# Feed-forward up and gate products: the two rounded parts of the tokens side by side as one 512-column moving operand, the halves added on the way out

## The chip, the cores and the metric

The kernel runs on one core of a Trainium2 chip. The metric is the device time of one execution in microseconds. Engines are named as in the profile: PE is TensorE's matmul side, PEld its weight loads, ACT is ScalarE, DVE is VectorE, SP is SyncE, whose queue issues the loads from memory.

## The reference

Two transformer stacks run one after the other on 256 tokens of width 1024 (the second stack adds 16 meta tokens). The change touches only the feed-forward blocks of the first stack: two layers with two blocks each, four in all.

```python
D_MODEL = 1024; SEQ = 256; DEPTH = 2; D_FF = 2816

def swiglu(h, w_in, w_out):
    gate, up = jnp.split(h @ w_in, 2, axis=-1)
    return (jax.nn.silu(gate) * up) @ w_out
```

Everything is float32. The rest (token mixing with a gated delta rule and sparse attention, then attention, a recurrence and two mixtures of experts in the second stack) is left as it is.

## The kernel before

The program is a list of stages; the four feed-forward stages are called FFN 0 to FFN 3 here (from 36.8, 486.7, 686.4 and 1130.9 us of the span). All weights come as a stream of 1 MB slabs through a ring of `RING = 8` slots, and SP issues the load of slab i when the reader of slab i-8 has signalled. The ring and the order of the slabs are fixed by `slab_plan`.

A float32 product is made of three products of rounded operands (type fp32r): `w = w_hi + w_lo` and `v = v_hi + v_lo`, where the `hi` part is the value rounded by a copy and `lo` is what is left, and `w_hi*v_hi + w_hi*v_lo + w_lo*v_hi` is accumulated in PSUM. `thirds` issues these three matmuls (lines 1523, 1524, 1525), each with 128x128 weights and 256 moving columns (the tokens).

A feed-forward stage has `FFN_STEPS = 11` steps, and step t has 256 of the 2816 hidden columns. For each step:

- SP loads a `gate`, an `up` and a `down` slab, and 0, 1 or 2 `ada` slabs, which carry the modulation weights of later stages (FFN 0, 1 and 2 carry 16 of them: two in each of the steps 0 to 5, one in 6 to 9; FFN 3 carries 4).
- ACT rounds each of the three slabs (`split_hi`, L1673), DVE subtracts to get the low part (`split_lo`, L3123). DVE also sums the `ada` slabs (`sum_slab`, L739), two instructions and two short ones a slab, and thereby frees their slots (`ada_sum`).
- PE runs `up_split(t+1)` and then `down_split(t)`. `up_split` makes two units u = 2t and 2t+1 of 128 hidden columns; a unit is gate and up (j = 0, 1) over 8 pieces k of the width, 16 calls of `thirds`, 48 matmuls. `down_split` is 16 calls, 48 matmuls. So a step has 144 matmuls, a stage 1584.
- For each unit ACT computes silu of the gate half (L2155) and DVE multiplies it with the up half and splits the product (`hidden_split`, L3132, L3133, L3134), which signals `hid_done`.

PSUM has eight banks. Unit u uses bank u % 3, gate in columns 0 to 255 and up in 256 to 511; the sums of `down_split` stay in banks 3 to 6. The queues are in order, and DVE's order inside step a is: three `split_lo`, `hidden_split(a+1)`, the sums of the `ada` slabs of step a. ACT's is three `split_hi`, then the two silu. The slab order makes the `up` and `down` slabs of a later step wait for these sums: in the steps with two `ada` slabs, the load of the `down` slab that is split before `hidden_split(a+1)` is released by the second `ada_sum` after `hidden_split(a)`. The wait on PE in `up_split` is

```python
if u >= 3:
    pe.wait_ge(s["hid_done"], u - 2)
```

which is: unit u may start when unit u-3 has been read. `down_split(t)` waits for both units of its own step.

## Time and profile before

| | us |
|---|---|
| median of 3 runs | 2811.76 (2811.54 to 2816.03) |
| the profiled execution, its own time | 2810.16 |
| its span | 2808.3 |
| FFN 0, 1, 2, 3 on PE, first to last matmul of `thirds` | 36.8 to 229.5, 486.7 to 678.6, 686.4 to 876.9, 1130.9 to 1321.5 |

In the profile a line's mean duration of a matmul is longer than the distance between two starts, since matmuls are pipelined; the distance between starts is what counts in a stream.

### The profile page before, as it was taken

Reading aid. Unit: us, or ns where it says so; the run is one execution under the profiler, and the core shown is the slowest. Engines: PE = TensorE matmul, PEld = TensorE weight load, DVE = VectorE, ACT = ScalarE, POOL = GpSimd, SP = SyncE. Lnnn points to the kernel's source line nnn. Section 1 sums busy time; section 2 is a strip of 40 time slices with the busy share of each in tenths; the row PEclk is TensorE's granted clock in tenths of the full one; section 3 lists DMA queues with packets and bytes.
Section 4 is the critical chain, followed back from the end, with each engine's and each line's share of the span. In section 5 each row is a group of like instructions: output and inputs, shape, how many; then the busy total and the mean of one; then the engine's idle time right before and its main releaser. Section 6 shows DMA issues by size and latency. Waiting matters only on the chain.

```text
span 2808.3 us, 44780 instructions
## 1 busy us (share of the span) xinstructions
PE 2630.2 (94%) x18742; PEld 1900.3 (68%) x18742; DVE 1388.0 (49%) x2815; ACT 771.1 (27%) x1471; POOL 0.2 (0%) x4
## 2 busy tenths in 40 slices
PE   7999988999999988999999999999999999999998
PEld 6998867999999877999777533333357784333333
DVE  7875864786774774763233333333324541333333
ACT  3332443334342352442233211111012321111010
POOL 0000000000000000000000000000000000000000
PEclk8999989999999999999999999999999999999999
DMA  8776311675775411554211599999961237999997
GB/s 346 309 280 260 125 46 61 255 286 207 295 292 214 149 61 35 197 220 165 75 63 44 209 376 428 427 427 428 427 270 61 91 121 278 422 428 427 427 428 329
DMA packets 72353, 701.51 MB, mean 250 GB/s; under 512 B 8784, under 2 KB 11472, under 8 KB 11728
## 3 DMA queue, kind: packets, MB, share of 16 engines
q1 hardware_dynamic: 72144, 698.54, 62.1%
q8 instruction: 154, 2.52, 0.4%
q14 instruction: 55, 0.45, 0.0%
HBM read 697.46 MB, written 1.05 MB: 249 GB/s over the span
## 4 chain that ended last, share of the span: by engine, by line
PE 83%; DVE 7%; DMA 5%; ACT 3%; issue 2%; DVEq 0%; SPq 0%; ACTq 0%
PE ps L1326 14%; PE ps L832 11%; PE ps L1523 9%; PE ps L1525 9%; PE ps L1524 9%; PE ps L1351 7%; DMA ring<-slabs 5%; PE ps L1367 4%; PE ps L823 4%; PE ps L1079 2%; DVE x L2971 2%; PE ps L1502 1%; PE ps L814 1%; PE ps L799 1%; PE ps L1291 1%
## 5 line engine op out<-in xcount | busy, mean ns | idle before, releaser
L1523 PE MATMUL ps<-arena_parts 128*128 128x256 f32 x2112 | 600.4, 284 | 18.0 <-DVE arena_parts L3208 18.0
L1525 PE MATMUL ps<-arena_parts,ring_parts 128*128 128x256 f32 x2112 | 596.9, 283 | 0.0
L1524 PE MATMUL ps<-arena_parts 128*128 128x256 f32 x2112 | 595.0, 282 | 0.0
L1326 PE MATMUL ps<-ring,arena 128*64 128x512 f32 x2048 | 469.3, 599 | 43.3 <-ACT arena L2052 27.9
L1523 PEld LDWEIGHTS ps<-arena_parts 128*128 128x128 f32 x2112 | 399.7, 189 | 19.7 <-DVE ring_parts L3123 14.1
L1524 PEld LDWEIGHTS ps<-arena_parts 128*128 128x128 f32 x2112 | 402.2, 190 | 0.2
L1525 PEld LDWEIGHTS ps<-arena_parts,ring_parts 128*128 128x128 f32 x2112 | 398.9, 189 | 0.0
L1326 PEld LDWEIGHTS ps<-ring,arena 128*64 128x64 f32 x2048 | 148.5, 137 | 326.3 <-issue 248.3
L3123 DVE TENSOR_TENSOR ring_parts<-ring,arena_parts 128x2048 fp32r<-128x2048 f32 x132 | 300.8, 2290 | 112.4 <-ACT arena_parts L1673 112.1
L1673 ACT CAST arena_parts<-ring 128x2048 fp32r<-128x2048 f32 x132 | 250.1, 1905 | 301.0 <-DMA ring<-slabs 294.1
L832 PE MATMUL ps<-h,ring 128*128 128x256 f32 (+1 forms) x1408 | 327.2, 390 | 5.0 <-DVE h L3115 3.5
L832 PEld LDWEIGHTS ps<-h,ring 128*128 128x128 f32 x1408 | 265.6, 191 | 50.8 <-issue 6.6
L2950 DVE COPY arena<-ps 128x256 f32<-128x256 f32 x64 | 27.2, 425 | 457.7 <-PE ps L1335 457.7
L1351 PE MATMUL ps<-ring,arena 128*64 128x512 f32 x992 | 223.9, 593 | 0.0
L2046 ACT ACTIVATE arena<-ps 128x256 f32<-128x256 f32 x64 | 24.5, 383 | 663.9 <-PE ps L1326 663.9
L2971 DVE TENSOR_TENSOR x<-ps,x 128x544 f32<-128x544 f32 x256 | 173.6, 720 | 41.7 <-PE ps L1367 26.8
L1367 PE MATMUL ps<-arena 64*128 64x272 f32 x1024 | 163.0, 428 | 29.3 <-DVE x L2971 27.3
L739 DVE CUSTOM_DVE_ANT_0 ring<-ring,arena,vectors 128x1024 f32<-128x1024 f32 x144 | 177.0, 1280 | 10.9 <-DMA ring<-slabs 10.9
L1351 PEld LDWEIGHTS ps<-ring,arena 128*64 128x64 f32 x992 | 71.2, 137 | 139.4 <-issue 139.1
L1367 PEld LDWEIGHTS ps<-arena 64*128 64x128 f32 x1024 | 82.6, 185 | 94.6 <-DVE x L2971 75.8
L823 PE MATMUL ps<-ring,h 128*128 128x256 f32 (+3 forms) x576 | 115.0, 357 | 0.0
L823 PEld LDWEIGHTS ps<-ring,h 128*128 128x128 f32 (+1 forms) x576 | 84.5, 175 | 22.8 <-issue 2.6
(411 smaller groups left out, 2473.8 us busy)
## 6 DMA issues: line engine op xcount, KB each, us to landing
ring<-slabs SPq DMA_DIRECT2D x190, 2048.0 KB, 14.5
ring<-slabs SPq DMA_DIRECT2D x278, 1024.0 KB, 5.4
sq<-aside SPq DMA_DIRECT2D x2, 1024.0 KB, 7.9
arena<-aside SPq DMA_DIRECT2D x2, 1024.0 KB, 10.0
x<-xT SPq DMA_DIRECT2D x1, 1024.0 KB, 6.5
outT<-x SPq DMA_DIRECT2D x4, 256.0 KB, 2.7
constants<-const SPq DMA_DIRECT2D x1, 875.0 KB, 7.8
vectors<-vec SPq DMA_DIRECT2D x1, 647.5 KB, 7.3
```

What stands on the lines that cost most here:

```text
L739: ins = nc.vector.tensor_tensor_reduce(out=wt[:, f], in0=wt[:, f], in1=cond_row, scale=1.0, scalar=col("ada_b", l * NADA + n), op0=ALU.mul ...
L823: mm = nc.tensor.matmul(ps[0:size, b, 0:width], rhs[:, k, at:at + size], wt[:, k, c0:c0 + width], start=(k == 0), stop=(k == KC - 1))
L832: mm = nc.tensor.matmul(bank(b, n), wt[:, k, c0:c0 + P], rhs[:, k, 0:n], start=(k == ks[0]), stop=(k == ks[-1]))
L1326: mm = nc.tensor.matmul(ps[W * hh:W * hh + W, e % 2, :], rows_of, wt[:, c], start=(k == 0 and c == 0), stop=(k == 1 and c == 3))
L1351: mm = nc.tensor.matmul(ps[W * dh:W * dh + W, 3, :], hide[:, e % 2, j, W * hh:W * hh + W], wt[:, j, 512 * dh:512 * dh + 512], start=(hh == ...
L1367: mm = nc.tensor.matmul(ps[:, 4 + 2 * (i % 2) + dh, 0:T2], ysb[rows64, e % 2, i * P:(i + 1) * P], ge[rows64, e % 2], start=True, stop=True)
L1523: nc.tensor.matmul(out, w_hi, v_hi, start=start, stop=False, skip_group_check=True)
L1524: nc.tensor.matmul(out, w_hi, v_lo, start=False, stop=False, skip_group_check=True)
L1525: return nc.tensor.matmul(out, w_lo, v_hi, start=False, stop=stop, skip_group_check=True)
L1673: nc.scalar.copy(hi_slab(i), slab_view(i)).then_inc(s["w_hi"], 1)
L2971: nc.vector.tensor_tensor(two, ps[:, b:b + 2, 0:T2], two, ALU.add).then_inc(s["moe_x"], 4)
L3123: nc.vector.tensor_tensor(low_view(i), wt, hi_slab(i).bitcast(F32), ALU.subtract)\
```

## The change

The high and low token parts of one piece k are now neighbours in memory (`hh`), so that `w_hi` meets both in one matmul of 512 columns, which fills a bank: columns 0 to 255 hold the sum of `w_hi*v_hi`, columns 256 to 511 that of `w_hi*v_lo`. The third product, `w_lo*v_hi` with 256 columns, is accumulated on the second half. Gate and up now need a bank each, so that a unit has two banks and there are two pairs (banks 0 to 3); the sums of `down_split` move to banks 4 to 7. PE waits for unit u-2 where it waited for u-3. ACT copies both second halves of a unit out of PSUM (`lows`), DVE adds the halves of gate into `sil` and those of up into `hid`, ACT takes silu of the gate sum in SBUF, and DVE multiplies. `down_split` keeps its three products.

```diff
-                    if u >= 3:
-                        pe.wait_ge(s["hid_done"], u - 2)
+                    if u >= 2:
+                        pe.wait_ge(s["hid_done"], u - 1)
...
-                            mm = thirds(ps[:, u % 3, j * T1:j * T1 + n], hi[:, k, cols], lo[:, k, cols], hh_hi[:, k],
-                                        hh_lo[:, k], k == 0, k == KC - 1)
+                            b = 2 * (u % 2) + j
+                            nc.tensor.matmul(bank(b), hi[:, k, cols], hh[:, k].rearrange("p a n -> p (a n)"), start=(k == 0),
+                                             stop=False, skip_group_check=True)
+                            mm = nc.tensor.matmul(bank(b, T1), lo[:, k, cols], hh_hi[:, k], start=False, stop=(k == KC - 1),
+                                                  skip_group_check=True)
...
-                        mm = thirds(ps[:, 3 + d // 2, d % 2 * T1:d % 2 * T1 + n], hi[:, f, cols], lo[:, f, cols],
+                        mm = thirds(ps[:, 4 + d // 2, d % 2 * T1:d % 2 * T1 + n], hi[:, f, cols], lo[:, f, cols],
...
             def silu(u, par, n):
                 act.wait_ge(s["up_done"], u + 1)
-                nc.scalar.activation(sil[:, par, 0:n], ps[:, u % 3, 0:n], ACT.Silu).then_inc(s["silu_done"], 1)
+                nc.scalar.copy(lows[:, par], ps[:, 2 * par:2 * par + 2, T1:T1 + n]).then_inc(s["lows_out"], 1)
+                act.wait_ge(s["gate_sum"], u + 1)
+                nc.scalar.activation(sil[:, par, 0:n], sil[:, par, 0:n], ACT.Silu).then_inc(s["silu_done"], 1)
...
+                    g, b = sil[:, f, 0:n], 2 * f
+                    dve.wait_ge(s["lows_out"], u + 1)
+                    nc.vector.tensor_tensor(g, ps[:, b, 0:n], lows[:, f, 0], ALU.add).then_inc(s["gate_sum"], 1)
+                    link(nc.vector.tensor_tensor(v, ps[:, b + 1, 0:n], lows[:, f, 1], ALU.add))
                     dve.wait_ge(s["silu_done"], u + 1)
-                    link(nc.vector.tensor_tensor(v, sil[:, f, 0:n], ps[:, u % 3, T1:T1 + n], ALU.mult))
+                    link(nc.vector.tensor_tensor(v, v, g, ALU.mult))
                     link(nc.vector.tensor_copy(v_hi, v))
```

On DVE, in step 1 of FFN 0, after the three low parts, this stood before (`split_lo`, then `hidden_split` for two units, then the first `ada` sum; `sil` is silu of gate, `hid` the product, `arena_parts` its two parts):

```order
L3123 TENSOR_TENSOR ring_parts<-ring,arena_parts 128x2048 [waits w_hi] x3
L3132 TENSOR_TENSOR hid<-sil,ps 128x256 [waits silu_done]
L3133 CAST arena_parts<-hid 128x256 [waits dve_chain]
L3134 TENSOR_TENSOR arena_parts<-hid,arena_parts 128x256 [waits dve_chain]
L3132 TENSOR_TENSOR hid<-sil,ps 128x256 [waits silu_done]
L3133 CAST arena_parts<-hid 128x256 [waits dve_chain]
L3134 TENSOR_TENSOR arena_parts<-hid,arena_parts 128x256 [waits dve_chain]
L739 ISA ring,arena<-ring,arena,vectors 128x1024 [waits slot2_loaded]
```

At the same place of the changed kernel stands:

```order
L3130 TENSOR_TENSOR ring_parts<-ring,arena_parts 128x2048 [waits w_hi] x3
L3140 TENSOR_TENSOR sil<-ps,lows 128x256 [waits lows_out]
L3141 TENSOR_TENSOR hid<-ps,lows 128x256
L3143 TENSOR_TENSOR hid<-hid,sil 128x256 [waits silu_done,dve_chain]
L3144 CAST arena_parts<-hid 128x256 [waits dve_chain]
L3145 TENSOR_TENSOR arena_parts<-hid,arena_parts 128x256 [waits dve_chain]
L3140 TENSOR_TENSOR sil<-ps,lows 128x256 [waits lows_out]
L3141 TENSOR_TENSOR hid<-ps,lows 128x256
L3143 TENSOR_TENSOR hid<-hid,sil 128x256 [waits silu_done,dve_chain]
L3144 CAST arena_parts<-hid 128x256 [waits dve_chain]
L3145 TENSOR_TENSOR arena_parts<-hid,arena_parts 128x256 [waits dve_chain]
L741 ISA ring,arena<-ring,arena,vectors 128x1024 [waits slot2_loaded]
```

Each unit has two more instructions, and its multiplication waits for a silu that itself waits for the first of them. The sums of the `ada` slabs stand behind all of it.

On ACT, in the same step, the three casts of the slabs and the two silu were:

```order
L1673 CAST arena_parts<-ring 128x2048 [waits up_done,slot4_loaded]
L1673 CAST arena_parts<-ring 128x2048 [waits up_done,slot5_loaded]
L1673 CAST arena_parts<-ring 128x2048 [waits y_done,slot6_loaded]
L2155 ACTIVATE sil<-ps 128x256 [waits up_done,hid_done] x2
L1673 CAST arena_parts<-ring 128x2048 [waits up_done,slot1_loaded]
```

In the changed kernel a copy out of PSUM stands ahead of each silu, and the silu reads SBUF:

```order
L1678 CAST arena_parts<-ring 128x2048 [waits up_done,slot4_loaded]
L1678 CAST arena_parts<-ring 128x2048 [waits up_done,slot5_loaded]
L1678 CAST arena_parts<-ring 128x2048 [waits y_done,slot6_loaded]
L2160 COPY lows<-ps 128x512 [waits up_done,hid_done]
L2162 ACTIVATE sil<-sil 128x256 [waits gate_sum]
L2160 COPY lows<-ps 128x512 [waits up_done,hid_done]
L2162 ACTIVATE sil<-sil 128x256 [waits gate_sum]
L1678 CAST arena_parts<-ring 128x2048 [waits up_done,slot1_loaded]
```

The casts of the next step's slabs now stand behind a wait for DVE.

## Rows read from the trace of the kernel before

**Rows 1.** The page: busy time of PE, DVE and ACT over the span

```profile
PE 2630.2 (94%) x18742; PEld 1900.3 (68%) x18742; DVE 1388.0 (49%) x2815; ACT 771.1 (27%) x1471; POOL 0.2 (0%) x4
```

**Rows 2.** The page's groups: busy, mean ns of one, idle before and its releaser

```profile
L1523 PE MATMUL ps<-arena_parts 128*128 128x256 f32 x2112 | 600.4, 284 | 18.0 <-DVE arena_parts L3208 18.0
...
L1525 PE MATMUL ps<-arena_parts,ring_parts 128*128 128x256 f32 x2112 | 596.9, 283 | 0.0
...
L3123 DVE TENSOR_TENSOR ring_parts<-ring,arena_parts 128x2048 fp32r<-128x2048 f32 x132 | 300.8, 2290 | 112.4 <-ACT arena_parts L1673 112.1
L1673 ACT CAST arena_parts<-ring 128x2048 fp32r<-128x2048 f32 x132 | 250.1, 1905 | 301.0 <-DMA ring<-slabs 294.1
```

**Rows 3.** Windows of FFN 0 and FFN 3: width, busy of each engine, clock, DMA

```profile
core 0: us, PE busy (x) PEld busy (x) DVE busy (x) ACT busy (x) POOL busy (x), PEclk, DMA share, GB/s
60.00:200.00 140.00, 140.00 (x1179) 140.00 (x1178) 114.84 (x152) 52.30 (x45) 0.00 (x0) 1.00 0.74 286
1140.00:1310.00 170.00, 170.00 (x1430) 170.00 (x1429) 97.79 (x111) 60.73 (x50) 0.00 (x0) 1.00 0.54 205
```

**Rows 4.** Groups of PE from 36.8 to 102.0; then PE's timeline: start, us

```profile
L1523 PE MATMUL ps<-arena_parts 128*128 128x256 f32 x176 | 51.0, 290 | 13.7 <-DVE arena_parts L3208 13.7
...
102.12 0.28 PE L1523 MATMUL ps<-arena_parts 128*128 128x256 f32 x1
...
119.26 0.28 PE L1523 MATMUL ps<-arena_parts 128*128 128x256 f32 x1
```

**Rows 5.** PE's timeline at the start of FFN 0 and in the token mixing

```profile
38.26 0.41 PE L1523 MATMUL ps<-arena_parts 128*128 128x256 f32 x1
38.47 0.41 PE L1524 MATMUL ps<-arena_parts 128*128 128x256 f32 x1
...
235.39 9.95 PE L832 MATMUL ps<-h,ring 128*128 128x256 f32 x45 [0.77 <-ACT h L2150]
```

**Rows 6.** DVE's timeline over one step of FFN 0

```profile
118.53 0.43 DVE L3134 TENSOR_TENSOR arena_parts<-hid,arena_parts 128x256 fp32r<-128x256 f32 x1
...
120.00 1.28 DVE L739 CUSTOM_DVE_ANT_0 ring<-ring,arena,vectors 128x1024 f32<-128x1024 f32 x1
...
131.85 2.29 DVE L3123 TENSOR_TENSOR ring_parts<-ring,arena_parts 128x2048 fp32r<-128x2048 f32 x1 [0.17 <-ACT arena_parts L1673]
134.06 0.41 DVE L3132 TENSOR_TENSOR hid<-sil,ps 128x256 f32<-128x256 f32 x1
134.51 0.29 DVE L3133 CAST arena_parts<-hid 128x256 fp32r<-128x256 f32 x1
...
135.18 0.41 DVE L3132 TENSOR_TENSOR hid<-sil,ps 128x256 f32<-128x256 f32 x1
...
136.29 1.28 DVE L739 CUSTOM_DVE_ANT_0 ring<-ring,arena,vectors 128x1024 f32<-128x1024 f32 x1
```

**Rows 7.** SP's and ACT's timeline in that step: a load, its cast, the silu

```profile
124.93 0.33 SPq L547 DMA_DIRECT2D ring<-slabs  x1
...
129.91 1.91 ACT L1673 CAST arena_parts<-ring 128x2048 fp32r<-128x2048 f32 x1 [0.56 <-DMA ring<-slabs]
131.72 0.65 ACT L2155 ACTIVATE sil<-ps 128x256 f32<-128x256 f32 x2
```

**Rows 8.** Instructions that read PSUM: duration ns min/median/max, first and last start

```profile
L2155 ACT ACTIVATE sil<-ps x88: 368/378/388, 48.0 to 1308.6; 128x256 f32<-128x256 f32 x88
...
L2052 ACT COPY arena<-ps x64: 585/585/586, 1612.3 to 2799.4; 128x512 f32<-128x512 f32 x64
...
L2943 DVE TENSOR_TENSOR arena<-ps,arena x64: 424/425/426, 1599.9 to 2789.1; 128x256 f32<-128x256 f32 x64
```

**Rows 9.** PE's start of unit 8 and DVE's end of unit 6, FFN 1, then FFN 3

```profile
549.88 0.28 PE L1523 MATMUL ps<-arena_parts 128*128 128x256 f32 x1
...
549.68 0.42 DVE L3134 TENSOR_TENSOR arena_parts<-hid,arena_parts 128x256 fp32r<-128x256 f32 x1
...
1194.06 0.28 PE L1523 MATMUL ps<-arena_parts 128*128 128x256 f32 x1
...
1187.08 0.43 DVE L3134 TENSOR_TENSOR arena_parts<-hid,arena_parts 128x256 fp32r<-128x256 f32 x1
```

**Rows 10.** A down slab's load and its cast in FFN 1

```profile
572.43 0.33 SPq L547 DMA_DIRECT2D ring<-slabs  x1
...
578.66 1.91 ACT L1673 CAST arena_parts<-ring 128x2048 fp32r<-128x2048 f32 x1 [1.83 <-DMA ring<-slabs]
```

More of the change, by code:

```diff
@@ L464, in build @@
         sil = sb("sil", [P, 2, T2])
+        lows = sb("lows", [P, 2, 2, T1])
         const = sb("constants", [P, NCONST])
@@ L494, in build @@
             "h_hi", "h_lo",
-            "up_done", "silu_done", "hid_done", "y_done", "y_added", "aside_in", "proj_done", "proj_act",
+            "up_done", "lows_out", "gate_sum", "silu_done", "hid_done", "y_done", "y_added", "aside_in", "proj_done", "proj_act",
             "proj_dve", "rope_ready", "out_done", "pe_step", "act_step", "dve_step",
@@ L708, in build @@
         HH_HI = HI_W + HI_RING * SLAB
-        hh_hi, hh_lo = part(HH_HI, KC, T1), part(HH_HI + KC * T1, KC, T1)
+        hh = part(HH_HI, KC, 2, T1)
+        hh_hi, hh_lo = hh[:, :, 0], hh[:, :, 1]
         hid_hi, hid_lo = part(HH_HI + 2 * KC * T1, 2, 2, T1), part(HH_HI + (2 * KC + 4) * T1, 2, 2, T1)
@@ L3155, in y_add @@
                     xd = x[:, d, T2 - n:T2]
-                    ins = nc.vector.scalar_tensor_tensor(out=xd, in0=ps[:, 3 + d // 2, d % 2 * T1:d % 2 * T1 + n],
+                    ins = nc.vector.scalar_tensor_tensor(out=xd, in0=ps[:, 4 + d // 2, d % 2 * T1:d % 2 * T1 + n],
                                                          scalar=gate(d), in1=xd, op0=ALU.mult, op1=ALU.add)
```

## The prediction

> **What bounds the kernel now.** I read the page first. PE is busy 94% of the span, DVE 49% [rows 1]. The three lines of `thirds` are its largest group, 2112 matmuls each, and their idle time before is 18.0 us at the starts of the four stages and nothing elsewhere [rows 2]. So inside a feed-forward stage the time is PE's stream. The windows say the same: PE has no idle time at full clock in FFN 0 and in FFN 3. But they also show who comes next. In FFN 0 DVE is busy 114.84 of 140 us, in FFN 3 97.79 of 170 [rows 3].
>
> Then the timeline, for the rate. By 102.0 us of the span PE has issued 176 matmuls of each of the three lines, 528, which is 96 for step 0 and three times 144: the matmul at 102.12 opens unit 8. The one at 119.26 opens unit 10, since a step has 144. 17.14 us / 144 = 119.0 ns a matmul of 256 columns, 5.71 us a unit [rows 4]. At the start of FFN 0, at half clock, two starts lie 0.21 us apart [rows 5], that is 256 / 1.2 GHz = 213 ns: a column takes one cycle. At full clock 256 columns are 106.7 ns, so a matmul carries 12.3 ns beyond its columns.
>
> **What the change takes off PE.** In `up_split` 32 calls of `thirds` a step become 32 pairs of 512 and 256 columns, over 11 steps and 4 stages 1408. A call costs 3 x 119.0 = 357.1 ns. The pair is one of 256 columns, 119.0, and one of 512 columns of this type, which the trace doesn't show. If the 12.3 ns come once for an instruction, it takes 119.0 + 106.7 = 225.7 ns. If they belong to the columns, 2 x 119.0 = 238.1, and the pair gains nothing. The nearest row on the other side is L832, plain float32, which spends two cycles on each of 256 columns with one weight load: 45 of them in 9.95 us, the last lasting 0.38, so 9.57 / 44 = 217.5 ns [rows 5]; at that the pair costs 336.5, a gain of 20.6. I take 225.7, because it keeps what the rows show for one instruction and adds columns at their rate. The pair is 344.7, the gain 12.4 ns; bounds 0 and 20.6.
>
> For a step that is 32 x 12.4 = 0.40 us: 17.14 becomes 16.74. For a stage 352 x 12.4 = 4.4 us, for four 17.5.
>
> The Trainium skill, "TensorE: Matmul & The Clock Gate", section "Back-to-back issue gap", gives N/2.4 + 2.5 ns at full clock for an isolated gap, and adds that with weight loads the spacing is set by both. By its formula 256 columns take 109.2 and 512 take 215.8; the trace's 119.0 doesn't agree. A call would go from 327.5 to 324.9, a gain of 2.6 ns or 3.7 us in all. The measurement decides for the 256 columns.
>
> **What it adds on the other engines.** A unit gets an ACT copy of 512 elements out of PSUM, 0.585 us, and two DVE additions with one operand in PSUM, 0.41 to 0.43 each [rows 6, 8]. In DVE's order they lie ahead of the multiplication, and silu (0.378) waits for the first. The next instruction that depends on the one before starts 0.45 us after it (134.06 and 134.51) [rows 6]. So silu begins 0.45 after the first addition, ends 0.38 later, and the multiplication follows 0.04 later: 0.87 us, in which the second addition hides. For f = 0 the copy is free: ACT runs it while DVE does its last low part. For f = 1 it follows the first silu and has 1.1 us of DVE's work for its 0.585. A pair of units goes from 136.29 - 134.06 = 2.23 us to 2.23 + 1.74 = 3.97. PSUM traffic and the move of banks I cost at nothing: the y sums are read after the last step, and ACT has 0.5 us waits on the loads around every cast [rows 7].
>
> **Where this lands: a loop that doesn't contain PE.** In a step with two `ada` slabs the chain is: DVE sums them (120.00 on), the second sum releases a load at 124.93, its cast on ACT starts at 129.91 (4.98 later), DVE's low part at 131.85, the two units at 134.06, and the next sum starts at 136.29 [rows 6, 7]. That is 16.29 us against PE's 17.14: hidden, with 0.85 to spare. With the additions it is 18.03, and above PE's 16.74. Not every load is that fast: the twelve second-sum loads from step 2 to step 5 of FFN 0 to 2 took 4.98 to 6.75, mean 5.69 (one of them is the load at 572.43 with its cast at 578.66, 6.23) [rows 10]. Part of that is queueing behind loads that PE releases, which a longer step thins out. I take 18.3; bounds 18.03 and 18.7.
>
> Before, PE felt this loop little, since a unit waited for unit u-3. Now unit 2t+2 waits for unit 2t. In the trace before, the start of unit 10 in FFN 0 lies 119.26 - (118.53 + 0.43) = 0.30 us behind the end of unit 8 [rows 4, 6]; in FFN 1 unit 8 starts 0.22 us **before** unit 6 is done (549.88 against 550.10) [rows 9]. So there is no slack for an addition of 0.87 us a unit and a PE that comes earlier. Units 6, 8, 10, 12 and 14 have a margin from -0.2 to 1.6 us in FFN 0, 1 and 2; from unit 16 on it is over 2.6. In FFN 3, with four `ada` slabs in all, unit 8 has 1194.06 - 1187.51 = 6.55 us [rows 9], so nothing waits there. PE's wait on `hid_done` has its whole in-order stream queued behind it, the down products too; SP's loads and ACT wait for those, so the loop keeps its own pace.
>
> **Sum.** In each of FFN 0, 1 and 2 unit 6 waits for about 0.5 us (margin 0.4 to 0.7, less 0.87 and less part of PE's lead), and then four steps go at 18.3 instead of 16.74: 4 x 1.56 = 6.2. Together 6.7 us of new PE waits against 4.4 of gain: +2.3 a stage, +7.0 for three. FFN 3 gives -4.4. Sum +2.6 us on the profiled execution's own 2810.16; that execution lies 1.6 under the median, so 2811.76 + 2.6 = **2814.4 us**. The gain is real, and it is paid back as a wait.
>
> The ends. With 20.6 ns a call the step is 16.48, a stage gains 7.3 and waits 4 x 1.82 + 0.5 = 7.8: 3 x 0.5 - 7.3 = -5.8. With 0 ns it is 4 x 1.16 + 0.5 = 5.1 a stage, +15.4. The loop at 18.03 takes off 12 x 0.27 = 3.2, at 18.7 it adds 4.8. So from -9 to +20: 2803 to 2832.
>
> **Rivals.**
>
> *Streaming gains nothing* (chance 0.14): the 12.3 ns belong to the columns. For it: at half clock the excess is gone, which fits a supply of operands that is too slow only at full rate. Against: nothing in the rows shows a cost by column. 2811.8 + 15 = 2827.
>
> *The loop is heavier still* (0.14). ACT is held at the wait for the gate sum, and casts that could start stand behind it; or the loads queue at 5.7 us and more. For it: two engines now hand over three times a unit where it was once, and a late DVE holds ACT. Against: ACT's idle time on loads is long, 301 us over 132 casts [rows 2]. A further 0.9 us a step is 12 x 0.9 = 11 us: 2825. The point from which it decides is a step above 18.7 us.
>
> *The excess vanishes for the pair* (0.10), ends faster. The 12.3 ns are a collision of the next weight load with a short product, and a 512-column product hides it for both. The pair costs 217.5 and half of L832's, 108.8: 326, a gain of 31 ns. A stage gains 10.9 us, the step is 16.15, the waits 4 x 2.15 + 0.5 = 9.1. FFN 0 to 2 give -1.8 each, FFN 3 -10.9: -16.3, 2795. It decides from a pair under 333 ns on, where the sum passes -3. The Trainium skill's formula, quoted above, would give such a pair, 324.9 ns.
>
> *The loop doesn't bind* (0.07), ends faster. If the loads come early enough that the step stays under 16.8, the whole 17.5 are kept: 2794. It needs the additions to cost under 0.5 us a pair of units in place of 1.74, or the release of the loads to move ahead. Against it: the margins [rows 9].
>
> *My forecast* (0.55): a gain of 10 to 20 ns a call and 12 steps at 18.0 to 18.7, 2803 to 2822.
>
> **How the numbers follow.** A measurement of this kernel can tell 0.2%, 5.6 us, from no change. Faster by more: the two faster rivals, 0.17, and 0.01 of the forecast. Slower by more: the two slower rivals, 0.28, and 0.14 of the forecast. Within: 0.40. The range leaves out most of the two faster rivals (0.15) and little above: 2801 to 2829.
>
> **What the changed profile would show.** Distances on PE's timeline: 512 columns 225 ns, 256 columns 119. PE waiting in `up_split` for DVE's last instruction of `hidden_split` some 15 to 18 times, 1.5 us each and about 20 us in all, in FFN 0 to 2 at the even units 6 to 14, none beyond unit 2 in FFN 3. FFN 3 shorter by 4.4 us (190.6 to 186), FFN 0 to 2 longer by 2 to 3. From first multiplication to the end of the second unit on DVE, with the additions, 4.0 us. I am wrong if the pair isn't 345 ns, or if the steps with two `ada` slabs don't settle at 18.3; and if the 1.5 us pauses pull PE's clock down, everything behind them would be dearer.

## The result, and the profile after

One point of the description ahead first. It says that the third product, `w_lo*v_hi`, is accumulated on the second half of the bank. In the code it goes to `bank(b, T1)`, the first half, columns 0 to 255, where `w_hi*v_hi` stands; the second half holds `w_hi*v_lo` alone. The two additions outside PSUM are the same either way, and so is every step of the prediction.

| | before | after |
|---|---|---|
| median, us | 2813.36 | 2832.23 |
| lowest to highest, runs | 2811.54 to 2816.03, 4 | 2830.0 to 2835.1, 4 |
| ratio, 95% interval | | 1.0076, 1.0063 to 1.0089 |
| profiled execution: time, span | 2810.16, 2808.3 | 2831.81, 2830.0 |
| its mean granted clock of PE | 0.982 | 0.978 |

The kernel is slower by 0.76%, by the ratio of neighbouring runs; the medians differ by 18.9 us. (A fourth run of the kernel before moved its median from 2811.76 to 2813.36.) Forecast were 2814.4 and a range up to 2829: the sign of the point forecast is right, its size is not, and the median lies 3 us above the range.

The page after, busy time and groups (to be read against [rows 1, 2]):

```profile
PE 2634.3 (93%) x17334; PEld 1834.5 (65%) x17334; DVE 1452.6 (51%) x2991; ACT 824.8 (29%) x1559; POOL 0.2 (0%) x4
...
L1544 PE MATMUL ps<-arena_parts 128*128 128x512 f32 x1408 | 501.9, 399 | 33.9 <-DVE arena_parts L3145 17.1
...
L1546 PE MATMUL ps<-arena_parts,ring_parts 128*128 128x256 f32 x1408 | 395.6, 281 | 0.0
...
L3130 DVE TENSOR_TENSOR ring_parts<-ring,arena_parts 128x2048 fp32r<-128x2048 f32 x132 | 299.5, 2290 | 75.9 <-ACT arena_parts L1678 75.4
...
L1678 ACT CAST arena_parts<-ring 128x2048 fp32r<-128x2048 f32 x132 | 249.9, 1904 | 212.1 <-DMA ring<-slabs 209.0
```

PE issues 1408 instructions fewer, 18742 - 17334, but isn't busy for a shorter time. Its idle time ahead of the first product of `up_split` was 18.0 us at the four starts of the stages; it is 33.9 now, and 17.1 of it ends with L3145, the last instruction of `hidden_split`, the one that stands behind `hid_done`. ACT's idle time on loads falls from 294.1 to 209.0 and DVE's ahead of the low parts from 112.4 to 75.9: the loop has less room left than it had.

The windows of FFN 0 and of FFN 3 (width, busy of PE, PEld, DVE, ACT, POOL, clock, DMA share, GB/s; against [rows 3]):

```profile
60.00:200.00 140.00, 133.91 (x884) 122.06 (x883) 123.00 (x179) 60.52 (x59) 0.00 (x0) 1.00 0.75 285
...
1160.00:1330.00 170.00, 170.00 (x1118) 155.31 (x1117) 115.09 (x153) 73.67 (x72) 0.00 (x0) 1.00 0.54 206
```

In FFN 0 PE was busy for 140.00 of 140 us and now stands still for 6.1 of them; DVE is at 123.00 where it was at 114.84. FFN 3, where DVE has 17 us more than before too, has no gap.

PE's timeline at the start of two steps in FFN 2 (start, us, instruction, idle before and releaser), and a microsecond further on:

```profile
784.48 0.50 PE L1544 MATMUL ps<-arena_parts 128*128 128x512 f32 x1 [1.17 <-DVE arena_parts L3145]
...
803.32 0.50 PE L1544 MATMUL ps<-arena_parts 128*128 128x512 f32 x1 [1.78 <-DVE arena_parts L3145]
...
804.47 0.58 PE L1544 MATMUL ps<-arena_parts 128*128 128x512 f32 x1
804.85 0.41 PE L1546 MATMUL ps<-arena_parts,ring_parts 128*128 128x256 f32 x1
```

Units 10 and 12 start 18.84 us apart, [rows 4] had 17.14. PE doesn't set this distance: it waits 1.78 us at the end of it. Then the clock falls: the starts of the last two rows lie 0.38 apart, where in FFN 3 (below) such starts lie 0.23 apart. The window there:

```profile
804.00:808.00 4.00, 4.00 (x16) 3.42 (x14) 3.77 (x8) 0.06 (x1) 0.00 (x0) 0.57 0.48 195
```

0.57 is mostly the lower of the two levels, 1.2 GHz. Inside the stages there are three such stretches of 3.4 us that the kernel before doesn't have, at 579.2, 688.5 and 804.5 us. Each takes 1.7 us from PE.

What DVE does in that same step (to be read against [rows 6]):

```profile
782.24 0.42 DVE L3140 TENSOR_TENSOR sil<-ps,lows 128x256 f32<-128x256 f32 x1
782.57 0.41 DVE L3141 TENSOR_TENSOR hid<-ps,lows 128x256 f32<-128x256 f32 x1
783.21 0.43 DVE L3143 TENSOR_TENSOR hid<-hid,sil 128x256 f32<-128x256 f32 x1 [0.22 <-ACT sil L2162]
...
784.00 0.43 DVE L3145 TENSOR_TENSOR arena_parts<-hid,arena_parts 128x256 fp32r<-128x256 f32 x1
...
786.44 1.28 DVE L741 CUSTOM_DVE_ANT_0 ring<-ring,arena,vectors 128x1024 f32<-128x1024 f32 x1
...
798.88 2.29 DVE L3130 TENSOR_TENSOR ring_parts<-ring,arena_parts 128x2048 fp32r<-128x2048 f32 x1 [0.82 <-ACT arena_parts L1678]
801.08 0.42 DVE L3140 TENSOR_TENSOR sil<-ps,lows 128x256 f32<-128x256 f32 x1
```

The load and its cast, on SP and ACT:

```profile
791.37 0.33 SPq L548 DMA_DIRECT2D ring<-slabs  x1
...
796.94 1.91 ACT L1678 CAST arena_parts<-ring 128x2048 fp32r<-128x2048 f32 x1 [1.21 <-DMA ring<-slabs]
```

The chain is that of the prediction: two units of `hidden_split`, the sums from 786.44, the load at 791.37 that the second of them releases, its cast at 796.94, the last low part at 798.88, the next units at 801.08. The multiplication starts 0.97 us after the first addition (782.24 to 783.21), after an idle 0.22 behind the silu. From 782.24 to 801.08 are 18.84 us, the same as on PE: both go at the pace of this loop.

**Where the 21.7 us of span went.** From the starts of the first product of each stage and of the work behind it, in us:

| | before | after | difference |
|---|---|---|---|
| FFN 0 | 192.7 | 198.6 | +5.9 |
| FFN 1 | 191.8 | 199.8 | +8.0 |
| FFN 2 | 190.6 | 195.4 | +4.8 |
| FFN 3 | 190.6 | 188.2 | -2.4 |
| all outside the stages | 2042.6 | 2048.0 | +5.4 |

The steps of FFN 0 to 2, from the start of an even unit to that of the next, on PE; all were 17.14 before:

```
unit    2-4    4-6    6-8    8-10   10-12  12-14  14-16
FFN 0  16.91  17.47  18.21  19.24  18.20  18.53  17.07
FFN 1  16.85  18.00  18.26  19.60  18.49  17.91  17.07
FFN 2  17.00  17.75  18.21  18.39  18.85  18.59  16.97
```

The twelve steps between unit 6 and unit 14 take 18.54 on average. FFN 3's are all 16.81 to 16.98.

### The profile page after: what moved, and what is told of

Read it like the earlier page. It is cut to its first block, busy times and chain, and to the rows that moved or that the text cites. A ratio compares the mean times of both kernels' runs of the same rounds, so it can differ in the third digit from the quotient of the medians.

```text
span 2830.0 us, 42317 instructions
## 1 busy us (share of the span) xinstructions
PE 2634.3 (93%) x17334; PEld 1834.5 (65%) x17334; DVE 1452.6 (51%) x2991; ACT 824.8 (29%) x1559; POOL 0.2 (0%) x4
## 4 chain that ended last, share of the span: by engine, by line
PE 72%; DVE 13%; DMA 8%; ACT 5%; issue 2%; DVEq 0%; SPq 0%; ACTq 0%
PE ps L1328 14%; PE ps L834 11%; DMA ring<-slabs 8%; PE ps L1544 7%; PE ps L1353 7%; PE ps L1369 4%; PE ps L825 4%; PE ps L1546 4%; DVE ring L741 3%; DVE ring_parts L3130 2%; PE ps L1081 2%; PE ps L1527 2%; PE ps L1525 2%; PE ps L1526 2%; DVE x L2978 2%
## 5 line engine op out<-in xcount | busy, mean ns | idle before, releaser
L1544 PE MATMUL ps<-arena_parts 128*128 128x512 f32 x1408 | 501.9, 399 | 33.9 <-DVE arena_parts L3145 17.1
L3130 DVE TENSOR_TENSOR ring_parts<-ring,arena_parts 128x2048 fp32r<-128x2048 f32 x132 | 299.5, 2290 | 75.9 <-ACT arena_parts L1678 75.4
L1544 PEld LDWEIGHTS ps<-arena_parts 128*128 128x128 f32 x1408 | 266.6, 189 | 100.7 <-DVE arena_parts L3145 20.1
L1678 ACT CAST arena_parts<-ring 128x2048 fp32r<-128x2048 f32 x132 | 249.9, 1904 | 212.1 <-DMA ring<-slabs 209.0
L1546 PEld LDWEIGHTS ps<-arena_parts,ring_parts 128*128 128x128 f32 x1408 | 268.0, 190 | 0.0
L1525 PE MATMUL ps<-arena_parts 128*128 128x256 f32 x704 | 201.0, 285 | 0.0
L1526 PE MATMUL ps<-arena_parts 128*128 128x256 f32 x704 | 198.4, 282 | 0.0
L1525 PEld LDWEIGHTS ps<-arena_parts 128*128 128x128 f32 x704 | 133.3, 189 | 2.1
## 6 DMA issues: line engine op xcount, KB each, us to landing
ring<-slabs SPq DMA_DIRECT2D x190, 2048.0 KB, 14.7
```

The lines of the kernel that those rows point to most:

```text
L1525: nc.tensor.matmul(out, w_hi, v_hi, start=start, stop=False, skip_group_check=True)
L1526: nc.tensor.matmul(out, w_hi, v_lo, start=False, stop=False, skip_group_check=True)
L1544: nc.tensor.matmul(bank(b), hi[:, k, cols], hh[:, k].rearrange("p a n -> p (a n)"), start=(k == 0), stop=False, skip_group_check=True)
L1546: mm = nc.tensor.matmul(bank(b, T1), lo[:, k, cols], hh_hi[:, k], start=False, stop=(k == KC - 1), skip_group_check=True)
L1678: nc.scalar.copy(hi_slab(i), slab_view(i)).then_inc(s["w_hi"], 1)
L3130: nc.vector.tensor_tensor(low_view(i), wt, hi_slab(i).bitcast(F32), ALU.subtract)\
```

## The experiments

The runs come in three sets; each has its own runs of the kernel before on the same chip, with medians 2811.72, 2811.94 and 2811.67. Numbers behind a run are its median in us, the lowest and highest and the number of executions. Ratios are to the kernel before; they compare neighbouring runs, and can lie up to 0.2% off the quotient of the medians. "Stages" is the sum of the four feed-forward stages in the profiled execution, 765.7 before and 782.0 in the changed kernel.

**The changed kernel once more (after_again).** No edit.

> The changed kernel as it is, for a median beside the other runs of this call: 2828 to 2836 by every theory, with one to four stretches of 3.4 us at half clock inside FFN 0 to 2 that aren't in the kernel before.

2829.53 us (2829.32 to 2835.23, 4 runs), ratio 1.0068 (1.0052 to 1.0083). Stages 778.7, waits on `hid_done` 17.2 us in 14. Only one half-clock stretch lies inside the stages. So two profiles of one program differ in the stages by 3 us; what follows is read with that in mind.

**The ring alone (ring_of_two).** The kernel before, with two unit buffers in place of three and the closer wait.

```diff
-                    if u >= 3:
-                        pe.wait_ge(s["hid_done"], u - 2)
+                    if u >= 2:
+                        pe.wait_ge(s["hid_done"], u - 1)
...
-                            mm = thirds(ps[:, u % 3, j * T1:j * T1 + n], hi[:, k, cols], lo[:, k, cols], hh_hi[:, k],
+                            mm = thirds(ps[:, u % 2, j * T1:j * T1 + n], hi[:, k, cols], lo[:, k, cols], hh_hi[:, k],
```

> The kernel before, with only the PSUM depth of the change: two banks in turn for the units and PE waiting for unit u-2. Theory A (the loss comes from a longer DVE-ACT-DMA loop together with the closer wait; neither alone costs much): the margins in the trace before are -0.2 to 1.6 us, so a few waits under 0.3 us, 0 to +3 us. Theory B (the closer wait alone is the loss, because a stalled PE also releases its slabs late): +10 us or more.

2814.45 (2809.37 to 2818.63, 10), ratio 1.0011 (1.0001 to 1.0021). Stages 767.5, +1.8. One wait of 1.2 us, at unit 2 of FFN 0 and not at the units 6 to 14:

```profile
PE ps L1523 <- DVE arena_parts L3134: 1.2, 1, 1.2
```

Columns of this view: what waited, for what; us in all, times, longest. The closer wait costs next to nothing by itself.

**The additions alone (idle_additions).** The kernel before, three buffers and the far wait, with the copy, the wait of ACT and the two additions; the additions go to a spare buffer, and silu reads the copy of the gate in SBUF. The banks are those of before.

```diff
-                nc.scalar.activation(sil[:, par, 0:n], ps[:, u % 3, 0:n], ACT.Silu).then_inc(s["silu_done"], 1)
+                nc.scalar.copy(lows[:, par], ps[:, u % 3, :].rearrange("p (a n) -> p a n", a=2)).then_inc(s["lows_out"], 1)
+                act.wait_ge(s["gate_sum"], u + 1)
+                nc.scalar.activation(sil[:, par, 0:n], lows[:, par, 0], ACT.Silu).then_inc(s["silu_done"], 1)
...
+                    dve.wait_ge(s["lows_out"], u + 1)
+                    nc.vector.tensor_tensor(spare[:, 0], ps[:, u % 3, 0:n], lows[:, f, 0], ALU.add).then_inc(s["gate_sum"], 1)
+                    link(nc.vector.tensor_tensor(spare[:, 1], ps[:, u % 3, T1:T1 + n], lows[:, f, 1], ALU.add))
```

> The kernel before, with the change's copy, its wait for DVE and its two additions per unit as extra work whose results aren't used; the products and the three banks with PE's wait for unit u-3 stay. Theory A: the loop goes to 18.4 us a step in the steps with two ada slabs and the hidden units fall behind by some 6 us over five steps, of which the about 5 us between a unit's end on DVE and its next use on PE absorb most: 0 to +6 us. Theory C (the additions and the copies are the loss by themselves, whatever PE waits for): +15 us or more.

2814.71 (2813.07 to 2820.15, 10), ratio 1.0015 (1.0005 to 1.0025). Stages 770.2, +4.5, three waits:

```profile
PE ps L1525 <- DVE arena_parts L3141: 1.7, 3, 0.7
```

The pair of units takes 4.28 us on DVE, as in the changed kernel, and in the twelve steps of the loop DVE's units start 18.1 to 19.7 us apart, 18.7 on average, while PE keeps 17.14. The far wait leaves a whole unit more, 5.7 us, and four steps with an excess of 1.6 us each have used that up only at units 13 to 15, when the steps with two `ada` slabs are over.

**Both, without the wide product (three_of_256).** The changed kernel, its 512-column product taken apart into two of 256 into the same bank.

```diff
-                            nc.tensor.matmul(bank(b), hi[:, k, cols], hh[:, k].rearrange("p a n -> p (a n)"), start=(k == 0),
-                                             stop=False, skip_group_check=True)
+                            nc.tensor.matmul(bank(b, T1), hi[:, k, cols], hh_hi[:, k], start=(k == 0), stop=False,
+                                             skip_group_check=True)
+                            nc.tensor.matmul(ps[:, b, T1:2 * T1], hi[:, k, cols], hh_lo[:, k], start=False, stop=False,
+                                             skip_group_check=True)
```

> The changed kernel with the 512-column product made as two products of 256 columns into the same bank, all else as changed. If the wide product gains (distances after: 234 + 118 ns a pair where three took 357): FFN 3 goes from 188 back to 190.5 us, and in FFN 0 to 2 the steps that the loop doesn't bind get 0.2 us longer each, while the bound ones don't move: +3 to +7 us over the changed kernel. If the wide product is a part of the loss: less time than the changed kernel.

2840.35 (2830.54 to 2843.04, 4), ratio 1.0085 (1.0062 to 1.0108). Stages 789.7, +24.0; FFN 3 190.6, as before. Waits:

```profile
PE ps L1544 <- DVE arena_parts L3147: 16.4, 14, 2.8
```

This is the experiment that carries the verdict. The ring alone gave +1.8 in the stages, the additions alone +4.5, both together +24.0: 17.7 us belong to neither of them but to the two at once. (This kernel also has the moved banks; no_additions, next, has them too and is no slower for it.) The wide product then gives back 7.7 in the stages. In the whole time the kernel lies 8 to 11 us above the changed one by the medians and 2.5 to 5 by the ratios, where 3 to 7 were expected; four executions from 2830.5 to 2843.0 don't settle it closer.

**No additions (no_additions).** The changed kernel with banks, wide product and closer wait, without copy and additions. The second halves of the banks are computed and not used, so the product of high weights and low tokens is missing from the result.

```diff
-                nc.scalar.copy(lows[:, par], ps[:, 2 * par:2 * par + 2, T1:T1 + n]).then_inc(s["lows_out"], 1)
-                act.wait_ge(s["gate_sum"], u + 1)
-                nc.scalar.activation(sil[:, par, 0:n], sil[:, par, 0:n], ACT.Silu).then_inc(s["silu_done"], 1)
+                nc.scalar.activation(sil[:, par, 0:n], ps[:, 2 * par, 0:n], ACT.Silu).then_inc(s["silu_done"], 1)
...
-                    dve.wait_ge(s["lows_out"], u + 1)
-                    nc.vector.tensor_tensor(g, ps[:, b, 0:n], lows[:, f, 0], ALU.add).then_inc(s["gate_sum"], 1)
-                    link(nc.vector.tensor_tensor(v, ps[:, b + 1, 0:n], lows[:, f, 1], ALU.add))
                     dve.wait_ge(s["silu_done"], u + 1)
-                    link(nc.vector.tensor_tensor(v, v, g, ALU.mult))
+                    link(nc.vector.tensor_tensor(v, g, ps[:, b + 1, 0:n], ALU.mult))
```

> The changed kernel without the copy and the two additions: silu and the multiplication read the first halves from PSUM, so the product of high weights and low tokens is left out. Theory A: the loop is back at 16.3 us, PE sets the pace with steps of 16.9 us, FFN 0 to 3 last about 188 us each: 8 to 12 us under the kernel before, about 2803. Theory B or a theory that the 512-column products or the moved banks hurt: at or above the kernel before.

2807.07 (2802.91 to 2812.26, 10), ratio 0.9982 (0.9972 to 0.9992). Stages 758.5, -7.2. Four waits, 2.2 us in all:

```profile
PE ps L1544 <- DVE arena_parts L3140: 2.2, 4, 1.1
```

The moved banks and the wide product are both in this kernel, and it is faster than the kernel before: neither is the loss. But it is not the 2803 expected, 8 to 12 us under the kernel before, and far from the 17.5 us that 12.4 ns a call would give: it saved 5 us of its time and 7 in the stages. The price of the product says why. PE's timeline of the changed kernel in the middle of FFN 3:

```profile
1248.88 0.40 PE L1544 MATMUL ps<-arena_parts 128*128 128x512 f32 x1
1249.12 0.28 PE L1546 MATMUL ps<-arena_parts,ring_parts 128*128 128x256 f32 x1
1249.23 0.39 PE L1544 MATMUL ps<-arena_parts 128*128 128x512 f32 x1
1249.46 0.28 PE L1546 MATMUL ps<-arena_parts,ring_parts 128*128 128x256 f32 x1
1249.58 0.39 PE L1544 MATMUL ps<-arena_parts 128*128 128x512 f32 x1
```

A pair takes 0.35 us (1248.88, 1249.23, 1249.58). Over the stage 512 columns take 232.7 ns and the narrow one 117.4, together 350.0 against 357.1 for three: 7.1 ns a call, 10.0 us for 1408, of which the waits take 2.2.

**384 columns (width_384).** no_additions with its wide product cut short, to get a third point of price by width.

```diff
-                            nc.tensor.matmul(bank(b), hi[:, k, cols], hh[:, k].rearrange("p a n -> p (a n)"), start=(k == 0),
+                            nc.tensor.matmul(bank(b, 384), hi[:, k, cols], hh[:, k].rearrange("p a n -> p (a n)")[:, 0:384], start=(k == 0),
```

> The kernel without additions, with the wide product cut to 384 columns (its output leaves out a half of the low token parts, too): for the price of a product by its width. Distances between starts so far: 119 ns at 256 columns (12 over the columns' 106.7), 234 at 512 (21 over 213.3). If the excess goes by columns: 160 + 16 = 176. If it comes once an instruction and grows with 512 for another reason (a full bank): 172. Total some 15 to 22 us under the kernel without additions.

2759.36 (2755.19 to 2763.79, 4), ratio 0.9809 (0.9794 to 0.9824). On PE's timeline in FFN 3:

```profile
1182.67 0.34 PE L1544 MATMUL ps<-arena_parts 128*128 128x384 f32 x1
1182.84 0.28 PE L1546 MATMUL ps<-arena_parts,ring_parts 128*128 128x256 f32 x1
1182.96 0.34 PE L1544 MATMUL ps<-arena_parts 128*128 128x384 f32 x1
```

Over the stage the wide one takes 175.3 ns, the narrow one 116.6. So 256, 384 and 512 columns take 119.0 (in a row of three), 175.3 and 232.7; at 2.4 GHz the columns alone are 106.7, 160.0 and 213.3. What lies above is 12.3, 15.3 and 19.4. A straight line through the three has about 5 ns once for an instruction and 7 ns more with every 256 columns; that is a fit to three widths in different surroundings (a 256-column product beside a wider one has 10 to 11 ns above its columns), not a shown cause.

The total was expected 15 to 22 us under no_additions and lies 48 under it; that forecast was far off, since 57 ns less for each of 1408 products are 81 us, of which the waits on the loop keep a part. The loop shows itself here once more from the other side. With PE at 15.1 us a step and no additions at all, there are 16 waits:

```profile
PE ps L1544 <- DVE arena_parts L3140: 21.7, 16, 2.5
```

The steps from unit 4 to unit 14 take 15.8 to 17.9 there, 16.8 on average. The old loop, 16.29 in its fastest step [rows 6, 7], binds as soon as PE is faster than it.

**Smaller sums (tiny_sums).** The changed kernel, the sums over the `ada` slabs inside the feed-forward stages cut to 64 of 1024 columns; so the modulation sums are left incomplete.

```diff
-        def sum_slab(eng, i):
+        def sum_slab(eng, i, m=T1 * 4):
...
-                ins = nc.vector.tensor_tensor_reduce(out=wt[:, f], in0=wt[:, f], in1=cond_row, scale=1.0,
+                ins = nc.vector.tensor_tensor_reduce(out=wt[:, f, 0:m], in0=wt[:, f, 0:m], in1=cond_row[:, 0:m], scale=1.0,
...
-                            sum_slab(dve, slab_at[q] + share_slab(st[1], st[2], a) + i)
+                            sum_slab(dve, slab_at[q] + share_slab(st[1], st[2], a) + i, 64)
```

> The changed kernel with the sums of the ada slabs in the feed-forward stages cut to 64 of 1024 columns (the modulation sums are left incomplete). The slabs are still loaded and released by DVE. Theory A: the loop loses most of its 4.8 us of sums, no wait on PE is left in the steps, FFN 0 to 2 last 188 to 190 us: 2800 to 2810. If DVE's sums aren't in the chain, 2830 as in the changed kernel.

2810.79 (2805.05 to 2816.21, 10), ratio 0.9992 (0.9983 to 1.0001). Stages 763.1, waits:

```profile
PE ps L1544 <- DVE arena_parts L3145: 5.3, 10, 1.2
```

With all additions and the closer wait in place, some 4 us a step less of DVE's work in the loop take 19 us out of the stages. The total is at the upper end of what was expected, and the waits are not quite gone: ten are left, of 0.3 to 1.2 us.

**The same slabs, spread (spread_after, spread_before).** The function gives the number of `ada` slabs ahead of step k. It puts two in each of the steps 0 to 5 and one in 6 to 9; the table has the same 16, from step 2 on one and two by turns.

```diff
-    past = lambda k: first + (min(2 * k, k + n - 10, n) if n > 4 else min(k, n))
+    past = lambda k: first + ((0, 2, 4, 5, 7, 8, 10, 11, 13, 14, 16, 16)[k] if n > 4 else min(k, n))
```

> The changed kernel with the 16 ada slabs of FFN 0 to 2 placed 2, 2, 1, 2, 1, 2, 1, 2, 1, 2, 0 over the steps in place of six times 2, then 1. A step with one sum less has a loop 2.4 us shorter, so that two neighbours last 18.4 + 16.0 = 34.4 us against PE's 2 x 16.9 = 33.8. Theory A (the loop through DVE's sums binds): the waits on PE fall from about 8 us a stage to 1 or 2, FFN 0 to 2 last 190 to 192 us where they took 195 to 200: 2812 to 2818. A theory in which the additions or the bank layout cost by themselves: 2830 as before.

> The kernel before with the same spreading of the ada slabs. Every theory: PE sets the pace in all steps already, so no change, 0 within 3 us.

On the changed kernel: 2816.9 (2810.78 to 2823.11, 10), ratio 1.0018 (1.0005 to 1.0031), stages 765.4, waits 2.5 us in 3. On the kernel before: 2813.92 (2812.57 to 2815.81, 10), ratio 1.0006 (0.9997 to 1.0016), every step 17.14. No work was taken away, and 16.6 us of the stages came back. The kernel before, which doesn't feel the loop, gets nothing from it.

The spreading has a cost of its own at the end of FFN 1, in both kernels. Step 9 now has two `ada` slabs to sum in place of one. Those 2.4 us lie in DVE's queue ahead of its last additions into `x`, which start 2.5 us later (675.50, and 673.00 in the kernel before), and the squares `sq` wait for these. PE's first matmul on `sq`, in the kernel before and in spread_before:

```profile
674.58 1.13 PE L1502 MATMUL ps<-sq,constants 128*128 128x256 f32 x4 [0.97 <-ACT sq L2138]
```

```profile
677.09 1.25 PE L1502 MATMUL ps<-sq,constants 128*128 128x256 f32 x4 [3.38 <-ACT sq L2138]
```

From 678.0 on 3.4 us of half clock follow, and FFN 1 takes 195.8 us where it took 191.8. In spread_after it takes 195.7, and not the 190 to 192 expected.

**Banks released earlier (early_release).** PE waits for the second addition of unit u-2, after which nothing reads the unit's banks, in place of `hid_done`.

```diff
-                        pe.wait_ge(s["hid_done"], u - 1)
+                        pe.wait_ge(s["up_sum"], u - 1)
...
-                    link(nc.vector.tensor_tensor(v, ps[:, b + 1, 0:n], lows[:, f, 1], ALU.add))
+                    nc.vector.tensor_tensor(v, ps[:, b + 1, 0:n], lows[:, f, 1], ALU.add).then_inc(s["up_sum"], 1)
+                    dve.wait_ge(s["up_sum"], u + 1)
```

> The changed kernel, in which PE waits for the second addition of unit u-2 (its banks are read then) where it waited for the end of hidden_split, 1.2 us later. Theory A: the loop's own pace of 18.5 us stays, so the gain is not 1.2 us for each of the 14 waits (17 us) but about 1.2 to 2 us once a stage, plus pauses of PE that don't happen: 2822 to 2829. If PE were itself in the loop that binds, each step would be 1.2 us shorter: 2815.

2825.47 (2817.64 to 2829.91, 4), ratio 1.0055 (1.0034 to 1.0076), stages 772.7 (its profiled execution is the fastest of the four). Waits:

```profile
PE ps L1544 <- DVE hid L3141: 10.9, 9, 2.4
```

Five waits fewer, but the steps that wait still take 17.5 to 19.5. The waits begin later in the stage, and from unit 8 to 14 the pace is again that of the loop, 18.54 us a step (18.64 there in the changed kernel): were PE a part of it, each step would have become 1.2 us shorter.

**Pauses filled (filled_waits).** The changed kernel; PE runs three products of zeros (float32, 256 columns, added to a bank, 1.3 us) ahead of its wait in steps 3 to 7.

```diff
+                    if f == 0 and t < 33 and 3 <= t % FFN_STEPS <= 7:
+                        pe.wait_ge(s["zeroed"], 1)
+                        for _ in range(3):
+                            nc.tensor.matmul(bank(4, T1), ident, zeros[:], start=False, stop=False, skip_group_check=True)
```

> The changed kernel with three float32 products of a zero operand (1.3 us in all, added to a bank of the y sums) ahead of PE's wait in the steps 3 to 7 of FFN 0 to 2. If PE's pauses of over 2 us draw the half-clock stretches inside FFN 1 and 2 (3 of 3.4 us in the changed kernel's trace, 1.7 us of time each), these vanish: -2 to -5 us against the changed kernel. If the stretches don't come from the pauses: the same number of them, and 0 to +3 us.

2825.09 (2823.65 to 2827.91, 4), ratio 1.0052 (1.0035 to 1.0069), stages 777.6. FFN 2 of this kernel, then that of the changed one:

```profile
698.00:892.00 194.00, 193.87 (x1267) 177.23 (x1268) 154.70 (x219) 83.06 (x82) 0.00 (x0) 1.00 0.69 260
```

```profile
702.00:897.00 195.00, 190.30 (x1240) 173.20 (x1239) 153.91 (x218) 82.48 (x80) 0.00 (x0) 0.99 0.68 259
```

PE does more and the kernel is 4 to 7 us faster (2829.5 and 2832.2 down to 2825.1), where 2 to 5 were expected. No half-clock stretch is left within the steps of FFN 1 and 2, and their bound steps take 18.10, which is PE's own 16.88 and 1.22 of zeros. So without pauses and without half clock the loop there needs 18.1 at most. FFN 0 stays at 198.3.

**Spread and released early (spread_early).** The last two edits on the changed kernel together.

> The changed kernel with both: the ada slabs spread over the steps, and PE waiting for the second addition only. Each took most of the waits away by itself (5 waits over 0.5 us left with the spreading, 11 with the early release, 15 in the changed kernel). Theory A: no wait is left but the first of FFN 0; FFN 0 to 3 last 190, 188, 188, 188 us, 11 us under the kernel before in the four stages together: 2801 to 2808, with the stretches at half clock outside the stages as the uncertainty. If it isn't under 2810, the time of the stages outside must have grown.

2809.93 (2806.58 to 2817.11, 11), ratio 0.9999 (0.9989 to 1.0008). Stages 762.3, -3.4; no wait for `hidden_split` is left, all steps take 16.81 to 17.07. FFN 2 there:

```profile
685.00:873.00 188.00, 187.84 (x1238) 171.56 (x1237) 153.75 (x218) 82.43 (x80) 0.00 (x0) 1.00 0.70 265
```

Its time is above what was expected, by 2 to 9 us. It is the best form of this change that I have, and it is level with the kernel before, not faster. Most of the missing time is the end of FFN 1: that stage takes 195.0 us where 188 was expected, by the cost of the spreading told above. PE waits there for `sq`:

```profile
670.66 2.08 PE L1504 MATMUL ps<-sq,constants 128*128 128x256 f32 x4 [4.57 <-ACT sq L2143]
```

6.8 us of half clock, from 668.7 on, lie around it. A distribution that leaves step 9 one slab was not tried. The clock shows in the executions too: over its 11 runs the mean granted clock is 0.979 and over the 21 runs of the kernel before beside them 0.981. Below 1.00 that is 0.021 and 0.019 of 2810 us, 59 and 54 us: 5 us, of which the end of FFN 1 is a part.

## Why the prediction was right or wrong

**Right: the mechanism.** PE waits in `up_split` for L3145 14 times, 17.1 us, longest 2.4 (15 to 18 times and about 20 us were given): in FFN 0 to 2 at even units from 6 to 14, and once at unit 2 of FFN 0; none in FFN 3. The step that sets the pace has the predicted order on DVE, SP and ACT. The rival "the loop doesn't bind" fell with the waits, and "the excess vanishes" with the 350.0 ns. That the chain by itself and the wait by itself cost little, and that the two together cost 24, is shown by ring_of_two, idle_additions and three_of_256; that the sums of the `ada` slabs are in the loop by tiny_sums and spread_after.

**Wrong: the sizes.** The step that failed is the sum: the product of 512 columns was put at 225.7 ns and measured 232.7, the loop was put at 18.3 us and measured 18.54, and the clock had no term, though it cost about as much as either. The sum was +2.6 us, the span grew by 21.7. Of the 19.1 us missed:

- *The product of 512 columns*, taken at 225.7 ns, takes 232.7. The pair gains 7.1 ns in place of 12.4; a step is 16.91 and not 16.74. It matters only where PE sets the pace: 6 free steps in each of FFN 0 to 2 (18 x 0.17 = 3.1 us) and FFN 3 (-2.4 measured, -4.4 predicted, 2.0). 5.1 us. That the 12.3 ns come once for an instruction was wrong, that they belong to the columns as well: the measured excess of 19.4 lies between 12.3 and 24.6, a little nearer to the second. The bounds 0 and 20.6 held it.
- *The loop*, taken at 18.3 us, was 18.54 in its twelve steps: 2.9 us. Units 4 to 6 took 17.74 where I had 17.2 with its wait: 1.5 us. The cost of the additions is enough for it: a pair of units from first to last takes 4.29 and took 2.32, +1.97 and not +1.74, since each silu leaves DVE idle for 0.22 us (I had 0.87 from first addition to multiplication, it is 0.97). That is 0.23 in each of twelve steps, 2.8 us. With a load of 4.92 us from issue to cast the loop takes 18.21, as in six of the twelve steps on DVE's timeline. For slower loads 18.3 left 0.27 a step above 18.03; on average they needed half of it, and most of that in one step of FFN 1, 19.60 us long, whose `down` slab took 6.3 us:

```profile
565.48 0.33 SPq L548 DMA_DIRECT2D ring<-slabs  x1
...
571.80 1.91 ACT L1678 CAST arena_parts<-ring 128x2048 fp32r<-128x2048 f32 x1 [1.90 <-DMA ring<-slabs]
```

  The other long one, 19.24, is a step in FFN 0 that I hadn't looked at. Beside its slabs it computes the table of the rotary embedding:

```profile
101.44 0.42 DVE L3140 TENSOR_TENSOR sil<-ps,lows 128x256 f32<-128x256 f32 x1
...
105.64 1.28 DVE L741 CUSTOM_DVE_ANT_0 ring<-ring,arena,vectors 128x1024 f32<-128x1024 f32 x1
...
110.46 0.29 DVE L3181 CAST arena<-arena 128x256 f32<-128x256 int32 x1
...
114.07 6.69 DVE L3130 TENSOR_TENSOR ring_parts<-ring,arena_parts 128x2048 fp32r<-128x2048 f32 x3
120.68 0.42 DVE L3140 TENSOR_TENSOR sil<-ps,lows 128x256 f32<-128x256 f32 x1
```

  4.2 us of units, 4.8 of sums, 3.6 of table and 6.6 of low parts are 19.24, and DVE is idle only at the two silu. In this step no load and no cast matters; DVE is the bound by its own work. That is 0.9 us over 18.3.
- *The clock.* Nothing was put down for it, though the text said that pauses which pull it down would make everything behind them dearer. Of the three stretches at half clock in the stages, 1.7 us each, two lie in the steps counted above. The third, at 688.5, comes at the end of FFN 1 behind a wait for `sq`:

```profile
688.28 1.94 PE L1504 MATMUL ps<-sq,constants 128*128 128x256 f32 x4 [2.15 <-ACT sq L2143]
```

  It and that longer wait are +2.6 us. filled_waits speaks for the link between pauses and stretches: with the pauses shortened none is left in the steps of its profile, where the changed kernel had two in one profile and one in the other. Three profiles are few for this.
- *Outside the stages* +5.4 us, which the text had costed at nothing. The stretches at half clock there add up to 92.2 us before and 102.4 after; 10.2 us at half speed are the 5 us. Over many executions the same is seen: the kernel before has a mean clock of 0.981 in 64 runs (0.978 to 0.983), the changed one 0.978 and 0.979 in its two sets of 4. That is 6 to 8 us of a run, in the stages and outside. The additions alone (0.981) and the ring alone (0.981) don't have it; three_of_256 has it (0.979) without any wide product, and so has spread_early (0.979) without any wait; no_additions, tiny_sums and filled_waits lie between (0.980). In single profiles the time outside the stages is 2041 to 2044 us for the four kernels with three products a call in the old banks, and 2043 to 2052 for the ten built on the changed one, with 2051.4 for no_additions: if this is more than the scatter of single executions, it doesn't need the additions. What in the changed kernel lowers the clock outside the stages was not found, and stays open.
- The rest is 1.6 us, and most of it is the closer wait at unit 2 of FFN 0, for which the sum had no term: PE waits 1.24 us there, and the first step takes 14.82 us where it took 13.85. ring_of_two has the same wait, 1.2 us.

**The range.** The price of the product and the loop both lie inside the bounds given. With the two sizes measured the text's own sum is 12 x (18.54 - 16.91) + 3 x 0.5 - 4 x 2.5 = +11 us, 2823, which is inside the range too. What put the result outside is what had no term at all: the clock outside the stages, the end of FFN 1 and unit 2 of FFN 0. The two slower rivals, 2827 and 2825, came nearest in number and neither is what happened: the pair does gain, 7.1 ns, and the loop stays under the 18.7 from which the heavier loop decides. Its reason, casts held up behind the gate sum, isn't seen: ACT still waits for loads for most of its idle time ahead of the casts (209.0 of 212.1 us).

The Trainium skill, "TensorE: Matmul & The Clock Gate", section "Back-to-back issue gap", gives N/2.4 + 2.5 ns for the isolated gap of one product, 215.8 ns for 512 columns; the 232.7 measured here doesn't agree, nor do 175.3 for 384 (162.5). The excess over the columns isn't constant in these rows.

## What to carry to other kernels

When a change makes the bounding engine faster and puts work on the others, look for the loop that doesn't contain the bounding engine, and add up its period with the new work; a margin of one unit in a ring of buffers can hide a loop that is slower than the engine for a handful of steps, and the same edit that lengthens the loop may take that margin away. Neither half of this edit showed its cost alone. Where DVE's work is uneven over the steps, cost the fullest step by its own sum, and spread slabs that aren't urgent before giving up; but look at what the last steps feed, since a sum moved there cost 4 us at the end of FFN 1. Joining two products into a wider one saved 7 ns of 357 here, 2%: nearly all of what these products cost went by the column.

## What the runs showed of the hardware

- Price of a product of `fp32r` parts with its own 128 x 128 weight load, full clock: 119.0 ns for 256 columns in a row of three, 175.3 for 384, 232.7 for 512; a 256-column one beside a wider one 116.6 to 117.4. At half clock 256 columns took 213 ns [rows 5] and 512 took 427 (starts from 804.85 to 807.62 in the changed kernel), the bare columns: the excess shows only at full clock.
- PE's clock after a pause inside a full stream, in the profile of the changed kernel. After waits of 2.37 us (at 578.18), 2.15 (688.28) and 1.78 (803.32) came 3.4 us at half clock, 1.0, 0.2 and 1.2 us later. After one of 2.17 us (122.92) came none, and none after the waits of 1.31 and less. The same program had three such stretches in the stages in one execution and one in another, so the length of the pause alone doesn't decide it here.
- A DVE addition, the silu that waits for it and the multiplication that waits for the silu have 0.97 us from first start to last start, of which 0.42 and 0.42 are the addition and the silu; the rest, 0.13, is the two handovers.
